# The first mixer's low-rank and preparation stages made one, with key norms and mixed inputs moved into the input projection

## The reference

```python
xx = h_prev - h
xs = h[None] + xx[None] * mu[:, None, None, :]        # six mixed inputs
r, k, v = jnp.einsum('pbtd,pde->pbte', xs[:3], w_rkv)
xv, xw, xa, xg = xs[2], xs[3], xs[4], xs[5]
w = -jax.nn.softplus(-(w0 + jnp.tanh(xw @ w1) @ w2)) - 0.5
a = jax.nn.sigmoid(a0 + (xa @ a1) @ a2)
g = jax.nn.sigmoid(xg @ g1) @ g2
kk = heads(k * k_k)
kk = kk / jnp.maximum(jnp.sqrt(jnp.sum(kk * kk, -1, keepdims=True)), 1e-12)
k = k * (1 + (a - 1) * k_a)
decay = jnp.exp(-jnp.exp(heads(w)))
# scan over tokens with r, decay, k, v, -kk, kk * a; then
bonus = jnp.sum(rh * kh * r_k, -1, keepdims=True) * vh
```

## Time and profile before

| what | value |
|---|---|
| median of three runs | 1500.87 us |
| the profiled execution, its own time | 1502.7 us |
| its span | 1501.0 us |
| TensorE busy (matmul) | 94% |
| VectorE busy | 57% |
| ScalarE busy | 45% |
| GpSimd busy | 16% |
| the two stages that are made one | 120.05 to 177.72 us of the span |
| rwkv_mid | 177.72 to 317.88 us |

### The profile page before, as it was taken

The page is one execution under the profiler, slowest core; times in us unless marked ns, Lnnn a source line. Parts: engine busy times, 40 slices in busy tenths (PEclk is TensorE's granted clock), DMA queues, the critical chain, the costliest instruction groups (busy, mean ns, idle before and its releaser), DMA issues. The chain is left out here.

```text
span 1501.0 us, 18775 instructions
## 1 busy us (share of the span) xinstructions
PE 1407.5 (94%) x7494; PEld 1135.2 (76%) x7494; DVE 853.3 (57%) x1158; ACT 679.3 (45%) x992; POOL 233.0 (16%) x127
## 2 busy tenths in 40 slices
PE   6999899989999989889999998998999998999998
PEld 2685467967888877467788886887887788977887
DVE  0764685467555454546755446566545677645564
ACT  1442343136444353344643334654563657426562
POOL 0003443004000022120400000120001332500110
PEclk7899799989999999799999999999999999999999
DMA  9655457074656556635566535952542453007940
GB/s 343 206 196 160 166 200 278 1 245 122 211 180 210 180 183 204 229 112 168 169 192 200 184 137 148 198 177 83 184 162 74 156 173 107 29 29 193 226 143 29
DMA packets 159395, 247.17 MB, mean 165 GB/s; under 512 B 14086, under 2 KB 98026, under 8 KB 158796
## 3 DMA queue, kind: packets, MB, share of 16 engines
q1 hardware_dynamic: 157980, 239.60, 50.8%
q0 software_dynamic: 1328, 6.38, 1.2%
HBM read 244.85 MB, written 4.24 MB: 166 GB/s over the span
## 5 line engine op out<-in xcount | busy, mean ns | idle before, releaser
L199 DVE TENSOR_TENSOR w_lo<-w_raw,w_hi 128x2048 fp32r<-128x2048 f32 (+3 forms) x176 | 411.7, 2348 | 293.5 <-ACT w_hi L190 293.4
L211 PE MATMUL ps<-w_hi,act_hi 128*128 128x512 f32 (+4 forms) x1216 | 471.3, 388 | 13.3 <-DVE w_lo L199 4.7
L213 PE MATMUL ps<-w_hi,act_lo 128*128 128x512 f32 (+4 forms) x1216 | 461.9, 380 | 0.0
L212 PE MATMUL ps<-w_lo,act_hi 128*128 128x512 f32 (+4 forms) x1216 | 461.5, 380 | 0.0
L190 ACT CAST w_hi<-w_raw 128x2048 fp32r<-128x2048 f32 (+3 forms) x176 | 316.9, 1806 | 254.6 <-PE ps L213 209.8
L211 PEld LDWEIGHTS ps<-w_hi,act_hi 128*128 128x128 f32 x1216 | 229.9, 189 | 60.2 <-issue 14.8
L213 PEld LDWEIGHTS ps<-w_hi,act_lo 128*128 128x128 f32 x1216 | 229.5, 189 | 38.4
L212 PEld LDWEIGHTS ps<-w_lo,act_hi 128*128 128x128 f32 x1216 | 230.1, 189 | 34.5 <-issue 0.5
L320 PE MATMUL ps<-w_raw,condz 128*32 128x512 f32 x384 | 63.3, 766 | 18.7 <-DMA w_raw<-in_ada_w 14.7
L672 POOL TENSOR_TENSOR nstat<-nstat,con 128x1 f32<-128x1 f32 x8 | 5.4, 678 | 429.4 <-DVE nstat L667 429.4
L211 PE MATMUL ps<-w_hi,ffn_gh 128*128 128x512 f32 x176 | 69.1, 393 | 0.0
(11 more groups left out here) (489 smaller groups left out, 1798.2 us busy)
## 6 DMA issues: line engine op xcount, KB each, us to landing
w_raw<-in_ada_w SPq DMA_DIRECT2D x48, 1024.0 KB, 6.8
w_raw<-in_ffn_w_in SPq DMA_DIRECT2D x88, 512.0 KB, 4.8
w_raw<-in_fox_w_in SPq DMA_DIRECT2D x32, 912.0 KB, 8.7
w_raw<-in_ffn_w_out SPq DMA_DIRECT2D x20, 1024.0 KB, 5.0
w_raw<-in_rwkv_w_rkv SPq DMA_DIRECT2D x12, 1024.0 KB, 6.3
w_raw<-in_gla_w_in SPq DMA_DIRECT2D x10, 896.0 KB, 4.9
w_raw<-in_gdn_w_in SPq DMA_DIRECT2D x10, 896.0 KB, 4.9
w_raw<-in_fox_w_out SPq DMA_DIRECT2D x8, 1024.0 KB, 5.1
```

The source lines that it names most:

```text
L199: self.nc.vector.tensor_tensor(lo[:, s, 0:c["nk"], 0:c["width"]], self.raw[:, c["slot"], 0:c["nk"], 0:c["width"]], hi[:, s, 0:c["nk"], 0:c ...
L211: nc.tensor.matmul(out(t)[:, 0:w], xh[:, k, tok], hi[:, s, j, 0:w], start=start, stop=False)
L212: nc.tensor.matmul(out(t)[:, 0:w], xh[:, k, tok], lo[:, s, j, 0:w], start=False, stop=False)
L213: return nc.tensor.matmul(out(t)[:, 0:w], xl[:, k, tok], hi[:, s, j, 0:w], start=False, stop=stop)
```

## The change

The stages rwkv_lora and rwkv_prepare become one, `stage_rwkv_low`, in a new order. Parts of them move ahead into rwkv_in and parts behind into rwkv_mid:

- rwkv_in's VectorE now also multiplies `k * k_k`, squares, sums and bounds it (`keys`, during the v projection), and after the mix for `a` makes the mixes for the decay and the gate (in the free tiles `m.a`, `m.g`). `k_k` and `k_a` are loaded there.
- In `stage_rwkv_low` the down projections of `a` and decay alternate, the first in output rows 0 to 63, the second in rows 64 to 127. Decay is taken up before `a`. The scaling of `lw` on GpSimd goes; its factor is in the exponentials. The gate's last 32 columns and its up projection come after the cumulative sums.
- `kka` moves from GpSimd to VectorE. The end of the bonus (times `r_k`, and the sum) moves to the start of rwkv_mid.
- Ada items: 2 + 2 + 9 before; 3 + 10 now.

The diff, cut to its core:

```diff
 def stage_rwkv_in(...)
@@ sync
+            sp.dma_start(k_k[:, :], a["rwkv_k_k"].broadcast_to([P, D])).then_inc(sem("k_k"), 16)
+            sp.dma_start(k_a[:, :], a["rwkv_k_a"].broadcast_to([P, D])).then_inc(sem("k_a"), 16)
             core.issue(sp, chunks[-1]["g"] + 1 + NRAW)
@@ vector; keys(n) is called behind the split of chunk n
+            def keys(n):
+                if n == 2 * per + 2:
+                    dve.wait_ge(sem("k_k"), 16)
+                    dve.wait_ge(sem("taken"), 4 * NT)
+                    nc.vector.tensor_tensor(kk[:, :, :], m.k[:, :, :], bc_out(k_k[:, :], NT), ALU.mult).then_inc(sem("kk"), 1)
+                if n == 2 * per + 3:
+                    dve.wait_ge(sem("kk"), 1)
+                    nc.vector.tensor_tensor(flat(m.lw), flat(kk), flat(kk), ALU.mult).then_inc(sem("kk"), 1)
+                    dve.wait_ge(sem("kk"), 2)
+                    nc.vector.reduce_sum(st[:, 0:32], by_head(m.lw), axis=AX_X).then_inc(sem("kk"), 1)
+                    dve.wait_ge(sem("kk"), 3)
+                    nc.vector.tensor_scalar(st[:, 32:64], st[:, 0:32], 1e-24, None, ALU.max).then_inc(sem("kk"), 1)
             mixed(3)
+            mix(core, dve, sem, 3, dx, h, decay_in)
+            mix(core, dve, sem, 5, dx, h, gate_in)
+def stage_rwkv_low(core, m, w, xs, low_w, key, at, free, items):
...
+        def _(pe):
...
+            for k in range(KD):
+                nc.tensor.matmul(ps[0:64, 0, 0:T], a1[:, k, :], xs[:, k, :], start=(k == 0), stop=(k == KD - 1))
+                r = nc.tensor.matmul(ps[64:P, 1, 0:T], w1[:, k, :], decay_in[:, k, :], start=(k == 0), stop=(k == KD - 1))
+            r.then_inc(sem("down"), 1)
+            for k in range(KD):
+                r = nc.tensor.matmul(ps[:, 2, 0:T], g1[:, k, 0:P], gate_in[:, k, :], start=(k == 0), stop=(k == KD - 1))
...
+            cum(0)
+            pe.wait_ge(sem("up_out"), 8)
+            cum(1)
+            pe.wait_ge(sem("exps"), 2)
...
+            ada.pe_sums(pe, sem, 0)
+            pe.wait_ge(sem("g2"), 32)
+            pe.wait_ge(sem("low"), 4)
+            pe.wait_ge(sem("exps"), 6)
+            for t in range(NT):
+                tok = slice(t * P, t * P + P)
+                for c in range(2):
+                    up(8 + 2 * t + c, [(low[:, 2, 0, tok], g2[:, 0, :]), (low[0:32, 2, 1, tok], g2[0:32, 1, :])])
+            ada.pe_turn(pe, sem, 0)
+            for n in range(1, len(items)):
                 ada.pe_sums(pe, sem, n)
                 ada.pe_turn(pe, sem, n)
@@ vector
+            dve.wait_ge(sem("rn"), 1)
+            link(v.tensor_tensor(by_head(kn), by_head(kn), bc_in(st[:, 32:64], 64), ALU.mult))
             for t in range(NT):
+                dve.wait_ge(sem("up_out"), 6 + 2 * t)
+                link(v.scalar_tensor_tensor(scr[:, t, :], A[:, t, :], -1.0, k_a[:, :], ALU.add, ALU.mult))
+                link(v.scalar_tensor_tensor(K[:, t, :], scr[:, t, :], 1.0, K[:, t, :], ALU.add, ALU.mult))
+                v.tensor_tensor(A[:, t, :], A[:, t, :], kn[:, t, :], ALU.mult).then_inc(sem("out"), 1)
+                link(v.tensor_tensor(rk[:, t, :], R[:, t, :], K[:, t, :], ALU.mult))
                 dve.wait_ge(sem("exps"), 3 * t + 3)
...
 def stage_rwkv_mid(...)
@@ vector, first
+            v.tensor_tensor(rk[:, :, :], rk[:, :, :], bc_out(rows[:, 2, :], NT), ALU.mult).then_inc(sem("bonus"), 1)
+            dve.wait_ge(sem("bonus"), 1)
+            v.reduce_sum(w["bonus"][:, :], rk[:, :, :].rearrange("p i (h j) -> p (i h) j", j=64), axis=AX_X).then_inc(sem("bonus"), 1)
             v.memset(state[:, :, :], 0.0).then_inc(sem("state_zero"), 1)
 def rwkv(...)
-    stage_rwkv_lora(core, m, w, h, dx, xs, low_w, low_at, later[0:2])
-    stage_rwkv_prepare(core, m, w, later[2:4])
-    stage_rwkv_mid(core, m, w, later[4:])
+    stage_rwkv_low(core, m, w, xs, low_w, key, core.s1, m.free, later[0:3])
+    stage_rwkv_mid(core, m, w, later[3:])
```

More of the change, by code:

```diff
@@ L1336, in steps @@
                     split(chunks[n])
+                after(n)
         @block.sync
@@ L1409, in stage_rwkv_lora @@
     g2 = core.place("g2", [P, 2, D], at + 8192)
-    at += 16384
-    low = core.place("low", [P, 3, 2, T], at)
-    scr = core.place("scr", [P, NT, D], at + 6144)
-    assert at + 6144 + 8192 <= w["ada_at"]
-    ada = Ada(core, w["ada_at"], items, 3, 0, T)
-    with core.stage("rwkv_lora") as (block, sem):
+    low = core.place("low", [P, 3, 2, T], at + 16384)
+    ex = core.place("ex", [P, NT, D], at + 22528)
+    assert at + 22528 + 8192 <= w["rk_at"]
+    shrink = float(np.exp(-0.5))
+    ada = Ada(core, w["ada_at"], items, 3, 2)
@@ L1417, in _ @@
+    with core.stage("rwkv_low") as (block, sem):
         @block.sync
         def _(sp):
[L1419 to L1424 removed]
@@ L1518, in stage_rwkv_prepare, with up @@
[L1518 to L1533 removed]
+            def up(u, parts):
+                if u >= 4:
+                    pe.wait_ge(sem("up_out"), u - 3)
+                c = u % 2 * COLS
+                for n, (x, down) in enumerate(parts):
+                    r = nc.tensor.matmul(ps[:, 4 + u % 4, :], x, down[:, c:c + COLS], start=(n == 0), stop=(n == len(parts) - 1))
+                r.then_inc(sem("up"), 1)
@@ L1534, in _, with cum @@
+            def cum(t):
                 for i, tri in enumerate(("cum_in", "cum_ex")):
```

212 lines of the change are left out of this document (76 added, 136 removed).

## The result

| | median | range | runs |
|---|---|---|---|
| before | 1503.61 us | 1496.52 to 1508.98 | 20 |
| changed | 1507.98 us | 1500.20 to 1518.28 | 20 |

The ratio is 1.0038, 95% interval 1.0022 to 1.0055: about 5.7 us slower (the two medians are 4.4 apart), with the upper end of the interval just past the half per cent. The change alone, measured once more on another occasion (experiment `e12_change_again`), gave 1.0017, interval 1.0002 to 1.0031. The profiled execution of the changed kernel took 1507.94 us, with a span of 1506.2; that of before 1502.7 and 1501.0.

What follows compares the result with a forecast made beforehand. TensorE, its matmuls busy for 94% of the span, was taken as the bound. The terms summed to +2.2 us: 1504.9 on the profiled 1502.7, 1503.1 against the median 1.8 lower, so 1503; range 1495 to 1510.

Steps and rivals of the forecast that it cites:

- an even exchange: Main case for the whole kernel: gains and losses about cancel, within about -3 to +6 us; chance 0.60.
- term 8: End of rwkv_mid: the tenth ada item runs there with nothing hiding it, +4.0 us (3.0 to 5.5).
- Term 1: End of rwkv_in: VectorE's added work makes TensorE start the next stage later, +2.3 us (upper end +4.3).
- Term 2: Down projections of a and decay: alternating in two column halves they run at once, -4.0 us.
- Terms 3 to 5: Merged stage: one boundary less -0.6, one ada item fewer -3.0, last two items waiting on the ring +1.0 us.
- Term 6: TensorE's clock: the longer hole at rwkv_in's end and slow stretches, between 0 and +4, taken as +1.5 us.
- the rival in which it falls: Hole at rwkv_in's end drops the clock for all down projections, 7.3 us more there, 1510; chance 0.12.
- Term 7: Start of rwkv_mid: the bias table's load queues behind more weight chunks, 0 to 3, taken as +1.0 us.
- cost at nothing: Work priced at zero; in rwkv_mid, VectorE's moved passes and memsets fit before the first mask, 7.0 to 9.1 of 9.3 us.
- The signs of being wrong: A TensorE wait inside the new stage, or rwkv_mid's length changing by something besides the item and bias load.
- term 5: Merged stage's ring: the last two items follow each other and wait for a chunk, 0 to 2.6, taken as +1.0 us.

Runs made afterwards that it cites:

- e12_change_again, e12: The changed kernel as it is, measured once more against the kernel before: 1506.37 us, ratio 1.0017.
- e8: Changed kernel with early copy, an eighth-item move into the block inverse, and the gate's mix moved back to the merged stage's start: 1497.55 us, 0.9972.
- e6: Changed kernel with the a and decay down projections one after the other, each still in its half of the array: 1509.26 us, ratio 1.0042.
- e1: Changed kernel with four ada items in the merged stage and nine in rwkv_mid, instead of three and ten: 1505.06 us, ratio 0.9992.
- e3: Kernel before with ScalarE's copy of the seventh ada item's sums moved ahead of the block inverse's copies: 1501.70 us, ratio 0.9972.
- e2: Changed kernel with ScalarE's copy of the seventh ada item's sums moved ahead of the block inverse's copies: 1499.57 us, ratio 0.9967.
- e9: Changed kernel, copy left late, with three filler products on TensorE ahead of the last three ada items: 1503.10 us, ratio 1.0001.
- e11: Changed kernel with the early copy, the gate's mix at the merged stage's start, and four plus nine ada items: 1501.63 us, ratio 0.9978.
- e10: Changed kernel with the early copy and the gate's mix at the merged stage's start, three plus ten ada items: 1499.90 us, ratio 0.9983.
- e5: Kernel before with the early copy, and the eighth item's sums and seventh's turn moved into the block inverse: 1504.55 us, ratio 1.0026.

## Why the prediction was right, and where its terms were not

I forecast 1503 us, an even exchange, with the sum at +2.2 us on the profiled execution. The profile of the change gave +5.2 on the span (+5.6 on the path), that of e12 +0.1 (+6.2 on the path), the two measurements +5.7 and +2.6. The even exchange is what happened, on its slow side. Part of it is luck: term 8 cost 5.7 us more than I gave it, and the number held because rwkv_mid came out 2.1 us below its term and the rest 0.8 lower, and because the range was wide. The changed kernel's median lies 5.0 us above the 1503 I named; 2.7 of these come from the kernel before, whose median was 1503.61 over twenty runs and not the 1500.87 of three. By its terms, in the profiled execution:

- **Term 1, +2.3**: the start of the down projections moved from 1.42 to 3.45 us behind the last input product, +2.0; VectorE's 12.2 us of work in a gap of 10.2 came as counted, its end at 121.62 for a forecast 122.0. Shown by e8, where it goes when the gate's mix goes. The price of the product with the row was 2.28 and not 4.32.
- **Term 2, -4.0**: 3.6 us for both in place of 7.6. Shown, with e6 as its counter-case, in which 2.6 us of it go and some overlap is left.
- **Terms 3 to 5, -0.6, -3.0 and +1.0**: the stretch as a whole, with terms 1, 2 and 6, came out as the sum has it (-2.8 us): 59.1, 61.4 and 59.1 us in three profiles of its old form, 56.0 and 55.5 in the two of the change. But the parts are others. An item fewer was worth 5.6 to 6.1 us (e1 against both), so that with four items the merged stage (61.6, 61.6 and 61.7 in three profiles) is 0.2 to 2.6 us *longer* than the old two, in spite of term 2. Part of the reason stands in the rows: e1 waited 1.60 and 1.56 us for chunks there, the profile of before never and that of e3 once (1.58). The windows make it likely why: the merged order has all items behind the one-column matmuls, the ring full and the DMA engines idle until then, where the old order used two items between other work. The changed kernel, then the kernel before (the last columns are clock, DMA share, GB/s):

```profile
140.00:150.00 10.00, 10.00 (x56) 6.15 (x54) 7.42 (x8) 5.32 (x6) 0.00 (x0) 1.00 0.00 0
```

```profile
140.00:150.00 10.00, 10.00 (x41) 3.98 (x39) 5.47 (x2) 4.19 (x8) 8.49 (x2) 1.00 0.64 222
```

- **Term 6, +1.5**: the clock held over the hole in the first profile. Over all eight profiles of kernels with the long hole it fell there in six, for 3.4 or 6.8 us; in none of the six without it. In e2 the two projections then took 5.3 us (121.26 to 126.55) instead of 3.6, in e12 6.2 (118.10 to 124.33). So the rival in which it falls was no rare case, but its price is 1.7 to 2.6 us, less than the 7.3 I gave it. The hole is not all of the clock's part: over the whole stretch the granted clock was 0.91 for 56.0 us against 0.94 for 59.1 before, by my estimate 10 us at 1.2 GHz against 7. The Trainium skill, "TensorE: Matmul & The Clock Gate", Part 1, as cited in the prediction, spoke for this; six of the eight profiles agree, and in the other two the clock held, so not every longer hole was paid twice.
- **Term 7, +1.0, had the wrong sign.** The bias matmul began 6.6 us after its load's issue in the profile of before and 3.7 in that of the change: -2.9. But it was 3.7 also in e3, which is the kernel before at that place, and 5.0 in e12, which is the change. Over all profiles it was 6.6, 5.5 and 3.7 in the old form, 5.0 twice, 4.1 once and 3.7 eight times in the new. The load lands sooner or later from run to run; that the new form helps it is likely and not shown. And the stretch got only 1.1 us shorter by it (125.2 to 124.1), mostly for something that I had **cost at nothing** there. VectorE's two moved passes fit ahead of the first mask only when the bias load is late. In nine of the eleven profiles of the new form it was early enough, and there the first mask stood 6.9 us behind the first transpose, right behind VectorE's memsets, and the last at 20.8; in e3, the old form with the load equally early, they stood at 5.4 and 19.5. That is 1.3 us lost to the change. The mid column says the same where the clock was alike: 122.1 to 122.6 in e1, e6, e9 and e11 against 120.6 in e3, though e3 is the only profile of its kind.
- **Term 8, +4.0 (3.0 to 5.5), was mis-sized**: 9.7 us, and this is the step that failed. Over three profiles with ten items and the late copy the tail was 24.8, 23.0 and 23.4, over two with nine 15.0 and 18.3: 7 us on average. I counted the item's matmuls, left the wait of 3.36 us where it was, and took the chunk as hidden ("half of the sums before it"). But the ring has three slots. Behind the output product the ninth item's second chunk and the tenth's two had still to be fetched, each asked for only when a slot fell free, all of them after the late copy. In the first profile the last was asked for at 309.35 and used at 317.16, 7.8 us later, against 6.2 in the earlier trace rows, while the DMA engines were full (1.01 in the window at 310.9) after having been idle through the block inverse. With the copy early the term is 3.9 (e2 against e3), which is what I had forecast for a queue without that wait. Behind an early copy the tail with ten items is 18.4 instead of 23.9 in the mean of the two profiles of the change; by e9 (21.3), some 2.6 of these 5.5 us go with the clock and 2.9 with the late requests.

The signs of being wrong that I named were both seen, at small prices: TensorE waits inside the new stage (1.67 us for a chunk, which term 5 had at 1.0, and 0.70 twice for a copy), and rwkv_mid's length changed by VectorE's moved passes too.

What the change itself is worth, with the tail repaired on both sides: e3 196.5 us of path in the old form, e11 197.1, e2 197.9, e10 197.8 and e8 195.3 in the new, and ratios of 0.9967 to 0.9983 that don't differ. Merging the stages is worth nothing that these runs can tell. The one moved copy is worth 0.5 to 0.7% on the changed kernel (0.9967 against 1.0017 and 1.0038; 7.0 to 7.6 us of path). The kernel before with it measured 0.3% faster, of which its tail shows only 0.5 us. e2_early_copy and e8_gate_mix_late are faster than both kernels given, without being shown faster than the kernel before with the copy moved. What stays open is why e5 measured slower than its path, and where most of e3's gain comes from.

## What to carry to other kernels

Work that streams its operands through a small ring isn't priced by its instructions: count which chunks can be resident when it starts, when the instruction that frees each slot runs, and who that one waits for. A copy that stands late in another engine's list for no reason of data can hold a whole queue of transfers while the DMA engines idle. And before trusting a forecast of a term that rests on one wait in one profile, look whether that wait is there in a second profile.

## What was not expected of the hardware

- Where two engines read SBUF: the Trainium skill, "SBUF — State Buffer", Who interferes with whom, has a VectorE instruction with two inputs in SBUF wait in full for a GpSimd instruction that reads SBUF. In e8 eight such instructions took 3.26 us inside GpSimd's power of 5.48 us, as long as the 3.25 alone, and the power took 5.43 us without them. So the measurement decides here: the small power does not hold the ports for its duration, although the large GpSimd product of the earlier trace rows went with 4.32 us in place of 2.29, and another VectorE product took 3.98 beside a GpSimd instruction of 3.99.
- Much of the spread of the runs goes with the clock. Over 265 runs (the change, the twelve experiments and the three sets of the kernel before beside them), the deviation of a run's time from its set's mean goes with the deviation of its mean granted clock, with a correlation of -0.72: 5.9 us longer for each 0.01 less. The profiles of one kernel differ in the same way: a stretch at 1.2 GHz near the start of the program lasted 23.9 us in the profiles of before and of the change, 17.1 in those of e1, e2 and e3.
- Matmuls into the two column halves need not start in the order of the list: in e6_one_after_other the first record of `w1` starts at 125.81 and the last three of `a1`, ahead of it in the list, at 126.16 to 126.59.
